# Second mixer of a two-layer model: the softmax steps moved in among the projection units of V, and RoPE and lambda made at the program's start

## What is computed

```python
def diff_attn_mixer(x, positions, norm_g, w_qkv, q_g, k_g, ..., subln_g, w_out, lambda_init):
    h = rmsnorm(x, norm_g)
    q, k, v = jnp.split(h @ w_qkv, 3, axis=-1)
    q = partial_rope(rmsnorm(q, q_g), positions)      # (B, S, 8 heads, 2, 64)
    k = partial_rope(rmsnorm(k, k_g), positions)
    lam = exp(sum(lam_q1 * lam_k1)) - exp(sum(lam_q2 * lam_k2)) + lambda_init
    p = softmax(q k^T * scale)                        # two maps per head
    a = p[:, :, 0] - lam * p[:, :, 1]
    o = rmsnorm(a @ v, subln_g) * (1.0 - lambda_init) # v: 8 heads of 128
    return o @ w_out
```

## Time and profile before

| | |
|---|---|
| median of three runs | 1878.59 us |
| the profiled execution's own time | 1878.4 us |
| its span, first to last instruction | 1876.6 us |
| PE, matmuls | 1855.0 us busy, 99% |
| VectorE | 1425.0 us, 76% |
| ScalarE | 975.8 us, 52% |
| GpSimd | 105.9 us, 6% |
| chain that ended last | PE 93%, VectorE 4%, ScalarE 2% |
| mean granted clock of PE | 0.998 |

### The profile page before, as it was taken

The page is one execution under the profiler, slowest core; times in us unless marked ns, Lnnn a source line. Parts: engine busy times, 40 slices in busy tenths (PEclk is TensorE's granted clock), DMA queues, the critical chain, the costliest instruction groups (busy, mean ns, idle before and its releaser), DMA issues.

```text
span 1876.6 us, 32956 instructions
## 1 busy us (share of the span) xinstructions
PE 1855.0 (99%) x11258; PEld 1559.6 (83%) x11258; DVE 1425.0 (76%) x2625; ACT 975.8 (52%) x1395; POOL 105.9 (6%) x71
## 2 busy tenths in 40 slices
PE   8999999999999999999999999999999999999999
PEld 6778888888888888888876688888888888888887
DVE  5575688988888888655588756889888888885555
ACT  5465555555545444444566655565455444444443
POOL 0000341000000000000000013510000000000000
PEclk9999999999999999999999999999999999999999
DMA  6445455555555555555553254555555555555555
GB/s 230 135 135 169 158 179 190 183 176 178 173 170 168 174 178 179 190 192 191 198 167 125 90 169 162 181 183 191 174 173 176 170 169 171 177 179 191 196 192 171
DMA packets 89488, 326.16 MB, mean 174 GB/s; under 512 B 10064, under 2 KB 10192, under 8 KB 89040
## 3 DMA queue, kind: packets, MB, share of 16 engines
q1 hardware_dynamic: 88848, 323.00, 53.0%
q10 hardware_dynamic: 576, 2.33, 0.3%
HBM read 324.24 MB, written 1.05 MB: 173 GB/s over the span
## 4 chain that ended last, share of the span: by engine, by line
PE 93%; DVE 4%; ACT 2%; issue 0%; DMA 0%; ACTq 0%; DVEq 0%
PE ps L1492 25%; PE ps L1490 14%; PE ps L1736 13%; PE ps L1738 12%; PE ps L1737 12%; PE ps L1489 4%; PE ps L1684 3%; PE ps L1508 2%; PE ps L1510 2%; PE ps L1509 2%; DVE wl L828 1%; PE ps L1665 1%; PE ps L1628 1%; ACT big L754 0%; DVE hT L837 0%
## 5 line engine op out<-in xcount | busy, mean ns | idle before, releaser
L828 DVE TENSOR_TENSOR wl<-raw,wh 128x1024 fp32r<-128x1024 f32 x569 | 696.5, 1227 | 162.0 <-ACT wh L468 153.3
L468 ACT ACTIVATE wh<-raw 128x1024 fp32r<-128x1024 f32 x609 | 641.6, 1055 | 317.0 <-PE ps L1738 165.0
L1492 PE MATMUL ps<-hT,wh 128*128 128x512 f32 x2072 | 739.2, 396 | 0.0
L1490 PE MATMUL ps<-hT,wl 128*128 128x256 f32 x2368 | 613.3, 279 | 0.0
L1490 PEld LDWEIGHTS ps<-hT,wl 128*128 128x128 f32 x2368 | 446.8, 189 | 25.0
L1492 PEld LDWEIGHTS ps<-hT,wh 128*128 128x128 f32 x2072 | 389.7, 188 | 78.8
L1736 PE MATMUL ps<-wh,hT 128*128 128x512 f32 x1024 | 402.2, 393 | 0.3 <-DVE big L812 0.2
L1738 PE MATMUL ps<-wh,hT 128*128 128x512 f32 x1024 | 399.3, 390 | 0.0
L1737 PE MATMUL ps<-wl,hT 128*128 128x512 f32 x1024 | 398.7, 389 | 0.0
L1738 PEld LDWEIGHTS ps<-wh,hT 128*128 128x128 f32 x1024 | 192.3, 188 | 40.2
L1736 PEld LDWEIGHTS ps<-wh,hT 128*128 128x128 f32 x1024 | 192.4, 188 | 39.6 <-issue 0.9
(11 more groups left out here) (225 smaller groups left out, 1347.2 us busy)
## 6 DMA issues: line engine op xcount, KB each, us to landing
raw<-stream SPq DMA_DIRECT2D x612, 512.0 KB, 3.4
big<-keys ACTq DMA_DIRECT2D x2, 1024.0 KB, 8.4
x<-x_in SPq DMA_DIRECT2D x1, 1024.0 KB, 5.4
out<-x SPq DMA_DIRECT2D x4, 256.0 KB, 2.1
sm<-small ACTq DMA_DIRECT2D x1, 228.5 KB, 5.6
pos_i<-positions ACTq DMA_DIRECT2D x1, 1.0 KB, 6.5
```

Of the source, the lines that this page charges most:

```text
L468: act.activation(wh[:, r, :], raw[:, r, :], ACT.Copy).then_inc(high_ready, 1)
L828: dve.tensor_tensor(wl[:, r, :], raw[:, r, :], wh[:, r, :].bitcast(F32), ALU.subtract).then_inc(made_low(unit), 1)
L1490: pe.matmul(near, w_l[:, kd, :], hTh[:, kd, :], start=False, stop=False)
L1492: i = pe.matmul(wide, w_h[:, kd, :], both, start=False, stop=(kd == KD - 1))
```

## The change

Neither the arithmetic nor the number of weight units changes.

1. The columns of Q, K and V are streamed in the order 0, 2, 1, 3, 4, 5 (`QKV_BLOCKS`): Q and K of the first four heads, then of the others, then V.
2. The RoPE angles and the lambda sums (25 small VectorE instructions) stand at the very start of VectorE's program, ahead of `norm(0, 0)`, behind the wait for `loaded_small`. The angles' sine is taken by ScalarE in the first feed-forward's query unit 2, lambda's exponentials in unit 5, and three small VectorE instructions of lambda follow in unit 8. Their results live in a new tile `rope` and in `lam`.
3. In a Q/K block VectorE now makes one unit's low part before the mean, one after it, one within `qk_norm`, and `qk_norm` is of the same block, not of the one before. ScalarE no longer changes its table in the first block.
4. PE turns part 0 ahead of block 2, part 1 ahead of block 3, part 2 ahead of block 4, part 3 in the last unit of block 4.
5. The 16 softmax steps stand between pieces of the V units (`STEP_AT`): pieces are counted from 0 at block 4, step j comes before piece 12 + 5j/4, so steps 0 to 3 are in the last unit of block 4 and 4 to 15 in the four units of block 5. The `keep_warm` of each step is gone. In step j PE holds scores j, turn j-3, and values j-4 for the first eight; values 8 to 15 come after the last unit. The turned maps go to a single bank (4) up to n = 12, and each has its own place in SBUF (16 places for 2). Products of two steps share bank 5 and are copied out at once (`da_got`), in VectorE's steps 6, 8, 10 and 12; values 2, 4 and 6 wait for the copy before (`o_got`).
6. `ahead` stands at the beginning of each step on ScalarE and VectorE, so the first step in each V unit makes the high and low part of the unit three on, before its maxima.

```diff
@@ -65,6 +65,7 @@
+QKV_BLOCKS = 0, 2, 1, 3, 4, 5
@@ -328,7 +331,9 @@
-        QKT_BEFORE = (3, 0), (4, 0), (5, 0), (5, 2)
+        QKT_BANKS = (0, 1), (2, 3), (0, 1), (6, 7)
+        QKT_LAST_AT = 15
+        STEP_AT = tuple(12 + 5 * j // 4 for j in range(16))
@@ -611,6 +620,12 @@
+                    if l == 0 and u == 2:
+                        act.wait_ge(trig_step, 1)
+                        act.activation(rope[:], rope[:], ACT.Sin).then_inc(trig_step, 1)
+                    if l == 0 and u == 5:
+                        act.wait_ge(lam_ready, 1)
+                        act.activation(lam[:, 2:4], lam[:, 0:2], ACT.Exp).then_inc(lam_ready, 1)
@@ -887,9 +906,33 @@
+            dve.wait_ge(loaded_small, 32)
+            chain(dve.tensor_copy(trig[:, 0, :, 0], pos_i[:]))
...
             norm(0, 0)
@@ -1351,19 +1370,19 @@
-            for nb in range(6):
+            for nb in range(4):
                 tokens_made(dve, ahead, qkv_mm, "qkv", nb, 0)
...
+                dve.tensor_copy(QK[:, 0, cols], ps[:, 4 + 2 * (nb % 2), :]).then_inc(qkv_out_v, 1)
+                ahead(unit_of["qkv"] + 4 * nb + 4)
+                qk_mean(nb)
+                ahead(unit_of["qkv"] + 4 * nb + 5)
+                qk_norm(nb, unit_of["qkv"] + 4 * nb + 6)
@@ -1380,38 +1399,49 @@
+            for j in range(16):
+                if j == 4:
+                    v_got(4)
+                ahead(unit_of["qkv"] + 16 + STEP_AT[j] // 4)
+                da_max(j)
+                if j >= 1:
+                    da_sums(j - 1)
+                if j >= 2:
+                    da_difference(j - 2)
+                if j in (6, 8, 10, 12):
+                    da_got((j - 6) // 2)
@@ -1800,32 +1825,77 @@
+            def da_step(j):
+                if j == 4:
+                    da_turn(0)
+                da_scores(j)
+                if j >= 4:
+                    da_turn(j - 3)
+                if j == 5:
+                    da_values(0)
+                if 5 <= j < 12:
+                    da_values(j - 4)
+
+            def v_chunk(at_):
+                if at_ in STEP_AT:
+                    da_step(STEP_AT.index(at_))
+                if at_ == QKT_LAST_AT:
+                    qkt(3)
+                if at_ == 16:
+                    pe.wait_ge(qkt_out, 8)
...
+            for nb in range(6):
+                if 2 <= nb < 5:
+                    qkt(nb - 2)
```

More of the change, by code:

```diff
@@ L342, in on_pool, with aT_bank @@
         def on_pool(unit):
-            return any(0 <= unit - unit_of[f"u{l}"] < POOL_UNITS and unit % 2 == 1 for l in range(2))
+            return unit % 2 == 1 and any(0 <= unit - unit_of[f"u{l}"] < POOL_UNITS for l in range(2))
+        def aT_bank(n):
+            return 4 if n < 13 else 4 + n % 2
         def made_low(unit):
@@ L747, in _ @@
                 ahead(unit_of["qkv"] + 4 * nb + 5)
+            preload(ACT.Exp)
+            ahead(unit_of["qkv"] + 18)
             def da_exp(n):
@@ L1414, in _ @@
-            ahead(unit_of["wo1"])
+            for j in range(16):
+                if j == 4:
+                    v_got(4)
+                ahead(unit_of["qkv"] + 16 + STEP_AT[j] // 4)
+                da_max(j)
[5 more added lines that the diff above has]
+                    da_got((j - 6) // 2)
+            chain(dve.scalar_tensor_tensor(out=epsz[:, :, 0:4], in0=z0[:, :, 0:4], scalar=EPS, in1=z0[:, :, 0:4],
+                                           op0=ALU.mult, op1=ALU.mult))
@@ L1415, in _ @@
+            head_var(0, 1, 1.0, epsz)
+            da_sums(15)
+            v_got(5)
+            da_difference(14)
+            da_difference(15)
+            head_scale(0, 1)
+            for pair in range(2):
+                head_norm(o_da, pair)
+            ahead(unit_of["wo1"])
+            for pair in range(2):
+                heads_transposed(4, pair, da_scale)
+            for k in range(2):
+                da_got_two(k)
+            ahead(unit_of["wo1"] + 1)
             chain(dve.scalar_tensor_tensor(out=epsz[:, :, 4:8], in0=z0[:, :, 4:8], scalar=EPS, in1=z0[:, :, 4:8],
@@ L1495, in up_both_halves, with token_unit @@
                 i.then_inc(used, 1)
-            def token_unit(unit, q, out, done, before=lambda t: None):
+            def token_unit(unit, q, out, done, before=lambda t: None, between=lambda t, k: None):
                 w_h, w_l = (w.rearrange("p (k c) -> p k c", k=2) for w in split(unit))
@@ L1504, in token_unit @@
                         kd = 2 * q + k
+                        between(t, k)
                         if t == 0:
@@ new lines, in qkv_bank @@
+            def qkv_bank(nb, t):
+                if nb >= 2:
+                    pe.wait_ge((qkv_out_v, qkv_out_a)[t], nb - 1)
+            for nb in range(6):
+                if 2 <= nb < 5:
+                    qkt(nb - 2)
+                for q in range(4):
+                    token_unit(unit_of["qkv"] + 4 * nb + q, q, lambda t: ps[:, 4 + 2 * (nb % 2) + t, :], qkv_mm,
+                               lambda t: qkv_bank(nb, t),
+                               lambda t, k: v_chunk(16 * (nb - 4) + 4 * q + 2 * t + k) if nb >= 4 else None)
@@ L1829, in _ @@
+            da_turn(13)
+            for n in range(8, 12):
+                da_values(n)
+            da_turn(14)
+            da_turn(15)
+            for pair in range(2):
+                head_transposes(4, pair)
+            for n in range(12, 16):
+                da_values(n)
+            out_projection(1, 4, ((pe_ready, 32), (hT_ready, 36)))
             ffn(1)
```

281 lines of the change are left out of this document (129 added, 152 removed).

## The result

The changed kernel takes 1899.74 us (median of 4 runs, 1898.52 to 1901.76) beside 1878.74 us of the kernel before on the same chip: ratio 1.0114, 95% interval 1.0096 to 1.0131. It is slower by 21.0 us. The forecast was 1899.1 us. The execution that was profiled is the longest of the four, 1901.76 us with a span of 1899.7 us, so the traces differ by 23.4 us (against 1878.4), 2.4 more than the medians.

What follows compares the result with a forecast made beforehand. PE, busy 99% of the span, was taken to bound the kernel. Terms 4.0 - 3.9 + 6.5 + 0.8 + 8.3 + 5.0 = +20.7 on 1878.4 gave 1899.1 us, eight-in-ten range 1884 to 1914.

Steps and rivals of the forecast that it cites:

- start: Program start: moved angles delay VectorE's first norm, +3.3 us, plus 0.7 for PE's clock (bounds 0 and 1.2): +4.0.
- RoPE gap and its half clock: Second mixer, behind the RoPE block: PE's 2.65 us wait and 1.2 us of half-clock matmuls go: -3.9 us.
- Q/K blocks and part 2's turns: Q/K blocks: VectorE's 13.9 us round makes PE wait 2.4, 2.1, 2.1 (+6.5); part 2's transposes moving ahead add +0.8.
- V stretch: Last unit of block 4 to output projection: +8.3 us for units and softmax steps, +5 for the clock.
- Rival 1: Faster: Q/K blocks stay under 11.8 us on VectorE and pieces fill PE's waits; 1870.0 us, chance 0.08.
- Rival 2: Q/K blocks are late but the V stretch breaks even, with no clock cost; 1885.8 us, chance 0.13.
- Rival 3: Clock stays low through the V stretch, +18 instead of +5; 1912 us, up to 1920; chance 0.14.
- Rival 4: Moved angles do not hold up the program's start: 3 to 4 us less, 1895, inside the forecast's own range.
- Four steps wait for high and low before their maxima: 6.4: V stretch, steps 4, 7, 10, 13: maxima wait for high 1.05 and low 1.22 instead of scores 0.7; 6.4 us.
- values wait: 3: V stretch, steps 6, 8, 10: values wait for VectorE's maxima, sums, difference and copy, about 1 us each; 3 us.
- four that cost, at the 1.2 above: 5: V stretch: of some six places where PE's clock may fall, four cost 1.2 us each; 5 us, bounds 0 and 18.
- VectorE's late arrival: V stretch: VectorE, still at the last block's RoPE, reaches the first maxima some 5 us after PE has the scores.

Runs made afterwards that it cites:

- experiment 1: Changed kernel with the RoPE angles and lambda sums moved from VectorE's start into the first feed-forward's query units: 1895.08 us, ratio 1.0092.
- experiment 7: Kernel before with only the RoPE angles and lambda sums moved, into the first feed-forward's query units: 1873.14 us, ratio 0.9979.
- experiment 2: Changed kernel with VectorE's old order in a Q/K block, the mean ahead of the low part: 1888.83 us, ratio 1.0066.
- experiment 4: Changed kernel with VectorE's copy of a head's product at the beginning of its step instead of the end: 1895.72 us, ratio 1.0094.
- experiment 5: Changed kernel with 15 idle matmuls on PE filling the wait ahead of scores 2: 1897.67 us, ratio 1.0105.
- kernel 8: Changed kernel with experiments 1, 2 and 4 together, and high and low parts at the end of each step: 1878.23 us, ratio 1.0003.
- experiment 9: Changed kernel with experiments 1, 2 and 4 together, high and low parts still ahead of the maxima: 1880.96 us, ratio 1.0022.
- experiment 12: Kernel 8 with ScalarE's output copy taken ahead of the exponentials: 1874.28 us, ratio 0.9983.
- experiment 6: Kernel before with only the RoPE angles and lambda sums moved, to the start of VectorE's program: 1876.66 us, ratio 0.9996.
- experiment 10: Kernel of experiment 7 with ScalarE's output copy taken ahead of the exponentials: 1870.48 us, ratio 0.9959.
- experiment 11: Kernel of experiment 10 without the idle warming matmul at the head of every softmax step: 1871.01 us, ratio 0.9965.
- experiment 3: Changed kernel with the one warming matmul back ahead of each of the 16 pairs of scores: 1902.16 us, ratio 1.0131.

## Why the prediction was right

It was right in the total and, against the traces, term by term to within 2 us; inside the last term it was not. In us:

```
term                           predicted   traces   how it was tested
start                              +4.0     +3.5    experiment 1: -4.1 (ratios), -4.7 (medians)
stretch 143 to 940 us               0       +1.2    not the change's, see below
RoPE gap and its half clock        -3.9     -4.4    experiment 7: -3.9 (ratios), -4.5 (medians)
Q/K blocks and part 2's turns      +7.3     +7.6    experiment 2: -6.6 in that stretch
V stretch                          +13.3    +15.1   in part: experiments 4, 5, 8 against 9, 12
sum                                +20.7    +23.0
```

The Q/K row is the measured +3.2 of the whole stretch with the gap's 4.4 taken off. The sum of 23.0 is the distance between the second feed-forward's starts (1096.52 and 1073.52). The medians are 21.0 apart. So part of the closeness of 1899.1 to 1899.74 is luck: the sum falls 2.3 short of the distance between the traces. Two small slips of reading change nothing: rows 2 are the longest wait of that stretch and not the only one (two more of 0.3 and 0.2 us), and 2.4, 2.1 and 2.1 make 6.6.

- *Start.* VectorE was free at 12.0 as forecast (11.84). The 0.7 added for the clock stands beside 0.4 (5.2 us behind the warming matmuls the clock from 12 to 17 us was 0.51, 1.00 before at 10 to 15; the turns' start moved by 3.0, what follows by 3.5). The choice between 0 and 1.2 was sound.
- *The gap.* The wait and the slow matmuls went. The two table changes cost PE nothing. The Trainium skill's page "ScalarE: Activation LUTs", section "What ACT_TABLE_LOAD costs", gives about 2.66 us for a change of tables, of which 1.28 are the load and 1.38 a drain. The trace agrees on the load, 1.28 us, and shows no drain: the load begins where the copy ahead of it ends (154.49 and 154.50), and the sine stands right behind it.
- *Q/K blocks.* VectorE's round was forecast at 13.9 us and is 13.87. Both idle times of VectorE, and what ends them, are as described. PE's delays were forecast at 2.4, 2.1, 2.1; the pace of the turns makes them 2.2, 2.1, 2.1, of which 4.3 in all are waits and the rest matmuls at the low clock. That this half clock costs nothing, since VectorE sets the pace, held.
- *V stretch.* The sum was about right and its split wasn't. "Four steps wait for high and low before their maxima: 6.4" and "values wait: 3" counted one chain twice, as the chain at 1045 us shows: the product's copy cost 4.0 (experiment 4), the high and low parts 2.7 (8 against 9), together 6.7 for 9.4. Set against it, "four that cost, at the 1.2 above: 5" had the count right, four falls of the clock in the trace, and the price too low: 2.5 us for the one that was measured. The other prices that the traces give are 1.3 us for 4.3 us at the low level (the V stretches of the changed kernel and experiment 1) and 1.1 for 3.3 (the steps of before and of experiments 6 and 7). At 0.3 to 0.42 us for each of the other 11.5 us, all four cost 6 to 7, an estimate; only the first was taken away by an experiment.
- *What the V stretch's sum lacks.* VectorE's late arrival was forecast at 5 us and is 4.45. With these sizes in place of the forecast ones the term would be 11 to 12 us and not 15.1, so some 3 to 4 us have no term. The largest waits are the turns' for ScalarE's copy of the map before, 6.6 us in four, and the list of the prediction has no line for them, apart from the 1.9 that carrying the queues forward added. Experiment 12, which puts that copy first, gained 4.0. That these are the missing microseconds is likely and not shown. The waits were forecast at 20 us in the whole and are 19.4, which is the size of the sum again and not its split.
- *Rival 1* (faster, 1870.0): it hung on a Q/K block staying under 11.8 us on VectorE. Experiment 2 makes it so, and the V stretch still takes 62.9 us. Only with every repair does the new order come to 1874.3; 1870.0 wasn't reached.
- *Rival 2* (V stretch breaks even): out, +15.1. It holds only for the kernel of experiment 12, with 51.8 us.
- *Rival 3* (low clock throughout): out, 17.5 of 67.4 us were at the low level. The page "TensorE: Matmul & The Clock Gate", section "HAM oscillation — how this bites in real kernels", of the Trainium skill has each short run begin cold; here waits in four places were followed by the low clock, and the 3.21 us wait that ended at 1049 us wasn't, so it came in some places and not in every one. In experiment 1, with the same instructions in the V stretch, the same wait (3.74 us there) was followed by it and the one of 2.37 us wasn't.
- *Rival 4* (angles don't hold the start): out, by the first rows above.

## What to carry to other kernels

Work put in front of a maximum, a mean or any link of a chain between three engines is paid by all that waits behind the chain, even where the engines that do it are idle half of the time (from 1020 to 1066 us VectorE was busy for 23.06 us and ScalarE for 24.13 of 46.00): ask for each filler which operand it waits for and who stands behind it. Here a change made to fill waits cost 21 us, and putting one copy ahead of the exponentials in the old order gave 2.7. Add up waits by chain and not by instruction, since parts of one chain are easily counted twice; and price a fall of the clock by the work that follows it, not by the wait that caused it.

## What the runs showed of the hardware

**The clock.** PE idle for 4.45 us was followed by 6 us at the low level. With 15 idle matmuls in that wait, in an execution in which 3.0 us of it were left, the clock was 1.00 behind it. The same kind of matmul issued once a step behind the waits left it at 0.89. Where the clock falls isn't fixed by the program: the same instructions had it low behind four places in one trace and three in another, and the old order's steps had one fall with the warming matmuls (before), none with them (experiments 6, 7 and 10) and one without (11). The last steps of experiment 7, where before has 0.53:

```profile
1041.00:1045.40 4.40, 3.10 (x23) 2.56 (x23) 3.11 (x10) 4.39 (x15) 0.00 (x0) 1.00 0.01 4
```

**A stretch that differs without a cause in the code.** Kernels 8 and 12 have the same instructions up to the second mixer's steps. The second mixer's warming matmuls begin at:

```profile
936.69 3.63 PE L1471 MATMUL ps<-ident_b 128*128 128x512 bf16 x16
```

in kernel 8, and in kernel 12 at:

```profile
935.46 3.63 PE L1471 MATMUL ps<-ident_b 128*128 128x512 bf16 x16
```

1.2 us lie between them, while the turns ahead of the query stage are within 0.1 us (139.88 and 139.95). ScalarE's activations in the two traces drift apart bit by bit, by 0.2 us at 393, 0.5 at 448, 0.8 at 497 and 1.1 at 546 us. Over all fourteen traces this stretch has one of two lengths: 796.7 to 796.8 us in the changed kernel and experiments 1, 5, 6, 8 and 9, 795.5 to 795.6 in before and experiments 2, 3, 4, 7, 10, 11 and 12, whether the angles were moved or not. Experiments 2, 3 and 4 have the instructions of the changed kernel up to there. So the 1.2 us of the table above aren't the change's; they come at a granted clock of 1.00 and without a wait of PE. They may be 1.2 of the 2.0 us by which the profiled execution of the changed kernel lies above its median, but each kernel was traced once, so whether the length changes from one execution to the next isn't shown. What causes it stays open.

The second feed-forward does the same on its own. From its first warming matmul to the end it takes 801.9 to 802.1 us in experiments 2, 3, 6, 7, 8, 9, 11 and 12 and 803.1 to 803.2 in before, the changed kernel and experiments 1, 4, 5 and 10. The two stages are long or short independently (6 has the first long and the second short, 10 the other way round), so two traces can differ by up to 2.4 us for this alone. That is why the terms above are read stretch by stretch, and not from whole spans. Open too is the exact price of the other three falls of the clock, which no run here filled.
